# Rounding the first half of the activations ahead of weight piece 10, and taking its remainder ahead of that of piece 9, in a mixture-of-experts loop on one core

## What is computed

```
def expert_block(args):
    xb, e = args
    g = xb @ w_gate[e] + b_gate[e]
    u = xb @ w_up[e] + b_up[e]
    g = jnp.minimum(g, SWIGLU_LIMIT)
    u = jnp.clip(u, -SWIGLU_LIMIT, SWIGLU_LIMIT)
    h = (u + 1) * (g * jax.nn.sigmoid(SWIGLU_ALPHA * g))
    return h @ w_down[e] + b_down[e]
```

## Time and profile before

| what | value |
|---|---|
| median of 3 runs | 1686.52 us (1685.93 to 1686.83) |
| the profiled execution, its own time | 1686.04 us |
| its span in the profile | 1684.0 us |
| TensorE busy | 1542.7 us, 92% |
| VectorE busy | 1270.2 us, 75% |
| ScalarE busy | 1045.1 us, 62% |
| the expert loop | from about 501 us to about 1658 us |

### The profile page before, as it was taken

The page is one execution under the profiler, slowest core; times in us unless marked ns, Lnnn a source line. Parts: engine busy times, 40 slices in busy tenths (PEclk is TensorE's granted clock), DMA queues, the critical chain, the costliest instruction groups (busy, mean ns, idle before and its releaser), DMA issues.

```text
span 1684.0 us, 21300 instructions
## 1 busy us (share of the span) xinstructions
PE 1542.7 (92%) x7091; PEld 1085.9 (64%) x7091; DVE 1270.2 (75%) x1256; ACT 1045.1 (62%) x950; POOL 171.8 (10%) x181
## 2 busy tenths in 40 slices
PE   2998977887949999999999999999999999999993
PEld 1998544554436767767676676767767677676762
DVE  5310354434348999998999999999998999998995
ACT  3331223333227777777787778777777787778775
POOL 1000001000150100001100001000001000001000
PEclk9999556557959999999999999999999999999997
DMA  7523122011048999999999999999999999999994
GB/s 244 125 92 112 34 30 68 1 35 51 27 175 304 360 365 379 367 367 369 357 372 374 373 369 363 370 362 376 371 368 370 353 373 375 373 368 359 371 356 172
DMA packets 170428, 464.24 MB, mean 276 GB/s; under 512 B 14196, under 2 KB 28152, under 8 KB 170120
## 3 DMA queue, kind: packets, MB, share of 16 engines
q1 hardware_dynamic: 149664, 423.72, 67.9%
q0 software_dynamic: 8880, 24.00, 6.1%
q10 hardware_dynamic: 11848, 16.09, 3.6%
HBM read 445.81 MB, written 23.58 MB: 279 GB/s over the span
## 4 chain that ended last, share of the span: by engine, by line
PE 65%; issue 12%; DVE 11%; ACT 5%; DMA 2%; DVEq 2%; ACTq 2%; POOLq 0%; POOL 0%; SPq 0%
PE ps L1433 61%; DVE ring_r L392 6%; PE ps L1436 4%; ACT ring_r L897 2%; DVEq L1402 1%; ACT reg_a L910 1%; DVE reg_b L1396 1%; DVE reg_b L1391 1%; DMA reg_p<-in_w_in 1%; DMA out_p_n<-reg_x 0%; POOLq L570 0%; DMA acc_rows<-reg_a,pass_tok 0%; DMA reg_x<-in_x_prompt 0%; DVE reg_w L1307 0%; ACT ring L958 0%
## 5 line engine op out<-in xcount | busy, mean ns | idle before, releaser
L1433 PE MATMUL ps<-ring_r,reg_z_r 128*96 128x512 f32 x4608 | 1099.7, 395 | 8.1 <-DVE reg_z_r L1361 7.1
L1433 PEld LDWEIGHTS ps<-ring_r,reg_z_r 128*96 128x96 f32 x4608 | 737.3, 162 | 323.0 <-DVE ring_r L392 11.4
L392 DVE TENSOR_TENSOR ring_r<-ring,ring_r 128x2048 fp32r<-128x2048 f32 x387 | 868.0, 2283 | 82.0 <-ACT ring_r L897 82.0
L897 ACT ACTIVATE ring_r<-ring 128x2048 fp32r<-128x2048 f32 x387 | 736.6, 1916 | 166.4 <-PE ps L1433 165.6
L592 POOL DMA_INDIRECT acc_rows<-reg_a,pass_tok x32 | 46.1, 1440 | 1029.9 <-issue 993.6
L1433 PE MATMUL ps<-reg_a_r,ring_r 128*128 128x260 f32 x576 | 106.5, 284 | 0.0
L916 ACT ACTIVATE reg_z_r<-ps 128x384 fp32r<-128x384 f32 x130 | 59.1, 480 | 65.9 <-PE ps L1436 65.9
L1433 PEld LDWEIGHTS ps<-reg_a_r,ring_r 128*128 128x128 f32 x576 | 89.6, 188 | 1.0 <-issue 0.9
L1433 PE MATMUL ps<-ring,reg_a 128*128 128x512 f32 (+1 forms) x160 | 83.3, 681 | 1.7 <-issue 0.9
L563 POOL DMA_INDIRECT reg_a<-xhat_rows,pass_tok x34 | 71.9, 2114 | 21.2 <-issue 21.2
L1361 DVE TENSOR_TENSOR reg_z_r<-ps,reg_z_r 128x384 fp32r<-128x384 f32 x130 | 65.7, 545 | 9.5 <-ACT reg_z_r L916 9.5
(11 more groups left out here) (284 smaller groups left out, 1069.2 us busy)
## 6 DMA issues: line engine op xcount, KB each, us to landing
ring<-in_w_gate SPq DMA_DIRECT2D x131, 1024.0 KB, 7.2
ring<-in_w_up SPq DMA_DIRECT2D x128, 1024.0 KB, 5.3
ring<-in_w_down SPq DMA_DIRECT2D x128, 1024.0 KB, 8.3
ring<-in_w_in SPq DMA_DIRECT2D x9, 1024.0 KB, 14.0
ring<-in_w_out SPq DMA_DIRECT2D x4, 1024.0 KB, 4.9
reg_x<-in_x_prompt SPq DMA_DIRECT2D x4, 512.0 KB, 4.8
reg_x<-in_x_prompt ACTq DMA_DIRECT2D x4, 512.0 KB, 4.0
xhat_rows<-reg_b ACTq DMA_DIRECT2D x4, 512.0 KB, 2.6
```

Of the source, the lines that this page charges most:

```text
L392: return eng.tensor_tensor(rest_r(k), w, rounded_r(k).bitcast(F32), ALU.subtract)
L897: act.activation(rounded_r(k), ring[:, slot_of(k), :], ACT.Copy).then_inc(hi_ready, 1)
L1433: return pe.matmul(out, lhsT, rhs, start=start, stop=stop, skip_group_check=True)
```

## The change

In the lists of ScalarE and VectorE two things change places, in both turns of the loop's body. ScalarE rounds half 0 of h before piece 10 instead of after it. VectorE takes the remainder of piece 9 after h half 1 instead of before the remainder of half 0, and the remainder of piece 10 after those of eX and half 1 instead of before them. No instruction is added or removed; TensorE's, SyncE's and GpSimd's lists stay as they are.

```diff
@@ ScalarE
-                            for n in range(8, 11):
+                            for n in range(8, 10):
                                 round_piece(k + n, p12, p48)
                             act.wait_ge(hT_psum2, t0 * 2 + (2 * u + 1))
                             round_blocks(eH, 0, 0, 1).then_inc(hhi_ready, 1)
-                            round_piece(k + 11, p12, p48)
+                            for n in range(10, 12):
+                                round_piece(k + n, p12, p48)
                             act.wait_ge(ex_psum, t0 + u + 2)
                             round_blocks(eX, 6, 0, 2).then_inc(xhi_ready, 1)
@@ VectorE
                                 dve.scalar_tensor_tensor(hrow[0:CAP, cs], hrow[0:CAP, cs], 1.0, eS[0:CAP, cs], ALU.add,
                                                          ALU.mult).then_inc(h_ready, 1)
-                                if q == 0:
-                                    rest_of_piece(k + 8, p12)
-                                rest_of_piece(k + 9 + q, p12)
+                                rest_of_piece(k + 8 + q, p12)
                                 if q == 0:
                                     dve.wait_ge(hhi_ready, t * 2 + 1)
                                     rest_of_blocks(eH, 0, 0, 1).then_inc(hlo_ready, 1)
...
                             rest_of_blocks(eX, 6, 0, 2).then_inc(ex_ready, 1)
                             dve.wait_ge(hhi_ready, t * 2 + 2)
                             rest_of_blocks(eH, 0, 1, 2).then_inc(hlo_ready, 1)
-                            for n in range(11, 15):
+                            for n in range(10, 15):
                                 rest_of_piece(k + n, p12)
```

## The result

| | before | changed |
|---|---|---|
| median | 1686.83 us (5 runs, 1685.93 to 1687.87) | 1706.12 us (5 runs, 1705.09 to 1706.39) |
| ratio | | 1.0114, 95% interval 1.0100 to 1.0128 |
| span of the profiled execution | 1684.0 us | 1704.3 us |

What follows compares the result with a forecast made beforehand. TensorE was taken to bound the loop. Product 10 starting 0.36 us later (u = 0) and 0.84 us later (u = 1), plus restart, made 1.34 us per pair, times 16 = 21.4 us: median 1707.9 us, range 1700 to 1714.

Steps and rivals of the forecast that it cites:

- Part 1: TensorE at product 8: its wait for half 0's remainder goes, worth 7.7 to 13.8 us alone.
- E: Zero point of the counted times in each expert: start of the 8 row transposes, where product 7 is over.
- Part 2: ScalarE: piece 10 is rounded later, covered by 0.83 us of idle time ahead of rounding 11; cost nothing.
- Part 3: VectorE waits for product 7, then pieces 9 and 10 come later; product 10 starts 1.20 us later per pair.
- Restart: TensorE at product 10: a product that waited may itself be longer, by 0 to 0.07 us; 0.07 taken.
- Not taken back later: VectorE behind product 10: 0.3 us earlier at piece 15's wait, nothing regained, so the loss repeats 32 times.
- Rival 4: VectorE falls behind over the whole expert, the room ahead of piece 15 being thin: 1713 us, chance 0.05.
- rival 3: VectorE's instructions stand end to end, chain 7.58 us rather than 7.24: 1718.8 us, chance 0.03.
- Rivals 1 and 2: At product 10: 1, only the removed wait counts, 1678.8 us, chance 0.06; 2, the two cancel, 1683 to 1690, chance 0.06.

Runs made afterwards that it cites:

- Experiment 7: Kernel before, with ScalarE rounding half 0 ahead of piece 10 and VectorE taking half 0's remainder between those of pieces 8 and 9: 1672.89 us, ratio 0.9924.
- experiments 1: Kernel before with ScalarE's half of the change alone, VectorE's list as before: 1686.38 us, ratio 1.0002.
- experiment 2: Changed kernel with ScalarE's list of before, so VectorE's half of the change alone: 1704.95 us, ratio 1.0108.
- experiment 5: Changed kernel with VectorE's list behind piece 9 in the order piece 10, half 1, eX: 1687.48 us, ratio 1.0002.
- experiment 3: Changed kernel with the remainder of piece 10 put back ahead of those of eX and half 1: 1706.69 us, ratio 1.0118.

## Why the prediction was right

The forecast's case happened, in sign, place and size: 1706.12 us against 1707.9, within the range.

- **Part 1 (the wait of product 8 goes)** held. Half 0's remainder ends 1.1 us before E, and product 8 starts at E + 0.60, near the floor of E + 0.56 rather than the E + 0.75 that the price of 7.7 us used. The wait of u = 1 was therefore real though no row named it: there too product 8 started 0.13 us behind the end of half 0's remainder (1069.72 + 0.55 against 1070.40), as in u = 0 (1034.56 against 1034.69). Experiment 7 prices part 1 alone at 12.9 us, near the upper bound of 13.8.
- **Part 2 (ScalarE, nothing)** held: experiments 1 and 2. Rounding 11 still starts at E + 0.20; the idle time ahead of it is 0.49 us of the 0.83. By the prediction's own times (1033.2 and 1033.66) some 0.46 us were to be left.
- **Part 3 (the chain from E)** held term by term: handover 0.20, h half 1 to piece 9 1.37 (1044.40 - 1043.03), piece 9 2.20, three activation remainders 1.40, piece 10 2.29, handover 0.04 (chain lines of the changed kernel). The sum is E + 7.50, as forecast. Product 9 starts at E + 3.91, 0.04 later than was taken for one without a stall of product 8; since product 8 began earlier than thought, its real stall is near 0.2 us (experiment 7, without it, has E + 3.72), and it is swallowed as said.
- **Restart** was a little too high. From product 10 to the next bias matmul it is 1055.95 - 1050.33 = 5.62 us against 2 x 2.79 = 5.58, so 0.04 us instead of 0.07. That makes 1.28 us per pair in place of 1.34, and 20.5 us in place of 21.4: 0.9 of the 1.8 us between forecast and median. Most of the rest is the step from the profiled execution to the median: the prediction put the median 0.48 us above it, and here it lies 0.27 us below (1706.12 against 1706.39). That step is scatter between executions; the only term that was mis-sized is the restart.
- **Not taken back later** held. VectorE's wait ahead of piece 15 in the turn u = 1 is 0.28 us in the changed profile, the 0.3 us that was left of 1.27 in the earlier trace rows. Rival 4, that it runs out, did not happen.
- **Instructions end to end (rival 3)** is ruled out by the chain: five steps take 7.26 us from 1043.03 to 1050.29, not 7.58. Read as end to end, the rule of the Trainium skill that was weighed there (VectorE: DVE Perf Modes, The DRAIN you can't avoid) would have given 1718.8 us. The same section of the Trainium skill adds that a next operation that is not held starts earlier, which the prediction left out. This trace shows the next start 0.08 us before the end of the row (1046.60 against 1044.40 + 2.28), as before the change.
- **Rivals 1 and 2** needed a chain 0.6 us shorter. None of it was.

What the prediction said of the changed profile was right but for three figures. It expected waits of 0.8 to 1.0 us in TensorE's list, and the matmuls show 0.57; the weight loads of the same product show 1.04. Counted from start to start, product 10 is 7.50 - (3.91 + 2.79) = 0.80 us late, between the two. It expected VectorE to be idle some 1.2 us ahead of the clip; that is so in u = 0 (1.29 us), but in u = 1 it is 1.71 us. And TensorE is busy 36.0 us in each window, not 35.7. None of the three enters the sum.

## What to carry to other kernels

When an item is moved in the list of an engine that works in order, look at the next wait on that same engine, and not only at the consumer that the item held up. Here piece 9 was the filler that kept VectorE busy until product 7 ended, and moving it behind that wait made everything from there to product 10 late. Count from the event that the list now hangs on, add up every item up to each later consumer (also the one after the next: experiment 5), and compare with when the engine that sets the time wants each result. Where the order of the items ahead of a consumer is changed but not which items they are, the wait only changes its name (experiment 3). Before believing an idle time, see whether the item behind it starts later; experiment 2 moved 1 us of it and changed nothing.

## What the runs showed of the hardware that was not expected

In these profiles the idle time ahead of the matmuls understates how late a product is, and can hide it: product 10 of the changed kernel is 0.80 us late and shows 0.57. Product 9 of the changed kernel is some 0.2 us late, with no idle time at the matmuls and 0.15 us at the weight loads; product 8 of u = 1 before the change started 0.15 us later than it does without a wait (E + 0.75 against E + 0.60), and no row showed a wait at all. The distance from start to start tells it better; the weight loads' waits at least name the late product in the changed kernel (0.15 and 1.04 us), but they overstate the longer one.
